# First panel pair behind two block norms on unnormalised tiles, the norm's factor applied to its results

## The chip, the cores and the metric

One core of one Trainium2 chip runs the whole program. The metric is the device time of one execution in microseconds (us). Each kernel is run several times and the median is compared.

## What is computed

Two transformer-like blocks work on 512 tokens of width 1024, in float32. The part that matters is in the second: a layer ends with a gated feed-forward block (down0 below), the next layer is a short convolution, and another feed-forward block follows (up1, down1). Each of them starts with a root-mean-square norm with a scale and a shift that come from a modulation vector:

```python
def rmsnorm(x, g):
    y = xf * lax.rsqrt(jnp.mean(xf * xf, axis=-1, keepdims=True) + NORM_EPS)
    return (y * g.astype(jnp.float32)).astype(x.dtype)

a = rmsnorm(h, norm1[i]) * (1.0 + sc1) + sh1
b_gate, c_gate, u = jnp.split(a @ w_in, 3, axis=-1)
h = h + g1 * ((b_gate * dwconv(c_gate * u, conv_w)) @ w_out)
n = rmsnorm(h, norm2[i]) * (1.0 + sc2) + sh2
g, u = jnp.split(n @ w_gate_up, 2, axis=-1)
h = h + g2 * ((jax.nn.silu(g) * u) @ w_down)
```

The factor of the norm belongs to the token, gain and scale to the channel of the input, so that (x * gain * (1 + scale) * r + shift) @ W = r * ((x * gain * (1 + scale)) @ W) + shift @ W.

## The kernel before, in words

All activations lie transposed: channels on the 128 partitions, tokens along the free axis. H holds the residual stream as 8 tiles of 128x512. A weight matrix is taken in panels of 128 output columns by up to 1024 input rows. Each panel is loaded by a DMA that SyncE issues into one of two slots of WS (`panel`, L667), and then split into a high and a low fp32r part: ScalarE copies (`split_panel`, L1508), VectorE subtracts (L2016), each in two halves of 128x512. SyncE loads a panel when both halves of the low split of the panel two before are done. Each product of float32 tiles is made of three fp32r matmuls: high input by low weights, low by high, high by high (`linear`, L854 to L867). A tile of output is 8 input tiles of 3 matmuls, 24 in all, or 66 in down0 and down1 with their 22 input tiles.

The order of the work is written out by hand, one program per engine with semaphores between them; there is no planner. `STAGES` (L48) lists the stages with their counts of panels and tiles. Around the change they are: up0 and down0, norm_e, conv_in (four passes of six panels: for j = 0 and 1 a c-gate panel, a u panel and a b-gate panel), conv_out (four passes of two), norm_f, up1 (22 passes of a gate panel and an up panel), down1. ada7a, ada7b and ada7c are modulation parts: VectorE multiplies and adds pieces of the modulation weights, TensorE sums the columns against ones (`add_beside`, L907, 8 matrix products that appear as 16 records), VectorE takes the result (`take_layer_part`, L2488).

A block norm runs as follows. For each of the 8 residual tiles VectorE updates H from the accumulator (L2474), ScalarE squares it (L1517), VectorE adds the squares up in SS (L2025). Behind the last one TensorE sums SS over the channels (`square_sum`, L914), ScalarE takes Ln and Exp (`root`, L1519) for the factor RS of each token, and `layer_norm` makes the eight normalised tiles: VectorE multiplies H by NS and RS (L2094), ScalarE adds the shift into the high part (L1554), VectorE makes the low part (L2088). The first two panels behind a norm go through `linear_pair` (L869): their weights lie in slots of their own (NH, NL), they use banks 2 and 3, and each normalised tile is multiplied by both panels as soon as it is there.

On VectorE, the low splits of the next stage's panels stand inside the queue of the stage's own work. In conv_in's first pass (L2749 on) VectorE, having made the norm, takes two modulation parts, clears CU, multiplies the two results of j = 0 (L2757), runs the three convolution taps (L2762, L2764), and only then splits panel 3. In up1's first pass it multiplies gate and up (L2730), makes the low part (L2732) and splits panel 3 at the head of the second pass. In down0 and conv_out, `residual_tile` (L2465) splits the next panel and then updates the residual tile.

Of the kernel before, what the change touches and what calls it, by code (L numbers as in the profile page):

```python
# [6 lines left out]
F32 = mybir.dt.float32  # L7
# [5 lines left out]
P = 128  # L13
# [54 lines left out]
    ("down0", 4, 6, 2, 0, 0),  # L68
    ("ada7a", 1, 0, 0, 1, 0),
    ("norm_e", 1, 0, 0, 1, 0),  # L70
    ("ada7b", 1, 0, 0, 1, 0),
    ("conv_in", 4, 6, 6, 0, 0),
    ("conv_out", 4, 2, 2, 0, 0),
    ("ada7c", 1, 0, 0, 1, 0),
    ("norm_f", 1, 0, 0, 1, 0),
# [244 lines left out]
def hybrid_then_diff_conv(nc, ins, consts, dist_rows, dist_table, out):  # L320
    with ExitStack() as ctx:
# [116 lines left out]
        A4H = sb("A4H", [P, KT, S], F32R, four)  # L438
        A4L = sb("A4L", [P, KT, S], F32R, four)
# [3 lines left out]
        YL = sb("YL", [P, KT, S], F32R, four)  # L443
        YT = sb("YT", [P, 2, S], F32, four)
        CU = sb("CU", [P, 2, S + 2], F32, four)
        CV = sb("CV", [P, 2, S], F32, four)
        four.close()
# [59 lines left out]
        f_hi, f_lo = sem("f_hi"), sem("f_lo")  # L507
        c_tap, cu_zero, out_kept, out_sent, last_sent = (sem(n) for n in ("c_tap", "cu_zero", "out_kept", "out_sent", "last_sent"))
# [308 lines left out]
        def _(pe):  # L817
# [51 lines left out]
            def linear_pair(a, hi, lo, base):  # L869
# [4 lines left out]
                for k in range(KT):  # L874
                    pe.wait_ge(ln_lo, base + k + 1)
                    for (wh, wl), b in tiles:
# [3 lines left out]
                        if k == KT - 1:  # L880
                            m.then_inc(w_used, 1)

# [558 lines left out]
            def ffn(l, count, base):  # L1441
                square_sum("norm_d" if l == 0 else "norm_f", count, 2 if l == 0 else 1)
                for a, _ in passes(pe, f"up{l}"):
                    if a.first():
                        linear_pair(a, A3H, A3L, base)
                    else:
                        linear(a, 0, 0, A3H, A3L)
                        linear(a, 1, 1, A3H, A3L)
# [31 lines left out]
            add_beside(At("ada7c"), 0, 12, SUM_BANKS[1])  # L1480
# [5 lines left out]
        def _(act):  # L1486
# [329 lines left out]
            def residual(stage, r, squared=True):  # L1816
                for a, more in passes(act, stage):
                    for t in range(2):
                        residual_tile(a, t, a.pg // 2, r, more, squared)
# [143 lines left out]
            def ffn(l, stage, L, shift, r, squared):  # L1963
                split(At(f"up{l}"), 1)
# [3 lines left out]
                for a, more in passes(act, f"up{l}"):  # L1968
                    if not a.first():
                        split(a, 1)  # L1970
                    panel_done(a, 0)
                    act.wait_ge(acc_free[acc(a, 1)], a.tile_round(1))
# [872 lines left out]
```

## Time and profile before

| | us |
|---|---|
| median of 3 runs | 1748.38 |
| lowest and highest | 1746.42, 1754.33 |
| the profiled execution | 1751.81 |
| its span in the trace | 1750.0 |
| TensorE busy | 1678.7 (96%) |
| VectorE busy | 976.1 (56%) |
| ScalarE busy | 678.1 (39%) |
| mean granted clock of TensorE | 0.976 of 2.4 GHz |

The span counts from the first to the last recorded instruction. Times in the trace are microseconds from the span's start. Where a row gives several instructions (x2), its duration is from the first's start to the last's end. The granted clock is in parts of 2.4 GHz: 1.00 is 2.4 GHz and 0.50 is 1.2 GHz.

### The profile page before, as it was taken

What the parts mean: (1) busy time and instruction counts of PE and PEld (TensorE: products, weight loads), DVE (VectorE), ACT (ScalarE), POOL (GpSimd) and SP (SyncE); (2) the same over time, 40 slices, a digit from 0 to 9 for tenths busy, and PEclk for the clock granted to TensorE, in tenths of its full rate; (3) what the DMA queues carried; (4) which work ended last, traced back from release to release, by engine and by line L of the source; (5) the groups of instructions that cost most, each with busy time, mean ns of one, the idle gap of its engine ahead of it and who ended that gap; (6) DMA issues with size and microseconds to landing.
All of it is one profiled execution on the core that took longest, in us unless ns stands there. A gap on an engine that the chain in (4) does not pass through costs nothing.

```text
span 1750.0 us, 22898 instructions
## 1 busy us (share of the span) xinstructions
PE 1678.7 (96%) x8888; PEld 1397.3 (80%) x8888; DVE 976.1 (56%) x1805; ACT 678.1 (39%) x1413; POOL 61.8 (4%) x120
## 2 busy tenths in 40 slices
PE   4899999999999999899999999999999899999999
PEld 2777777777999999777888888887888788888887
DVE  5667466766777766666555554345555533333332
ACT  3434556554455555554322323223222433333221
POOL 0000000000000000000000000000000000000000
PEclk9899998999999999998999999998999899999999
DMA  8886333313223131220666665433343233333332
GB/s 306 220 238 174 104 89 97 97 25 91 51 60 97 48 98 51 71 72 26 191 192 182 177 181 164 123 108 88 113 129 101 77 98 96 97 97 96 99 113 79
DMA packets 290215, 202.02 MB, mean 115 GB/s; under 512 B 76247, under 2 KB 272072, under 8 KB 289082
## 3 DMA queue, kind: packets, MB, share of 16 engines
q1 hardware_dynamic: 266942, 133.21, 27.3%
q0 software_dynamic: 15536, 56.37, 10.7%
q10 hardware_dynamic: 7628, 10.97, 1.9%
q8 instruction: 71, 1.16, 0.3%
q14 instruction: 38, 0.31, 0.1%
HBM read 197.33 MB, written 5.28 MB: 116 GB/s over the span
## 4 chain that ended last, share of the span: by engine, by line
PE 87%; DVE 6%; ACT 2%; issue 2%; DMA 2%; ACTq 1%; SPq 0%; DVEq 0%
PE PS L864 13%; PE PS L866 13%; PE PS L865 13%; PE PS L846 4%; PE PS L848 4%; PE PS L847 4%; PE PS L1285 3%; PE PS L1287 3%; PE PS L1286 3%; PE PS L1335 2%; PE PS L1094 2%; PE PS L1359 2%; PE PS L1068 1%; PE PS L1076 1%; PE PS L1347 1%
## 5 line engine op out<-in xcount | busy, mean ns | idle before, releaser
L2016 DVE TENSOR_TENSOR WL<-WS,WH 128x512 fp32r<-128x512 f32 x416 | 268.2, 687 | 256.5 <-ACT WH L1508 256.0
L1508 ACT ACTIVATE WH<-WS 128x512 fp32r<-128x512 f32 x416 | 237.8, 621 | 176.5 <-PE PS L848 135.0
L864 PE MATMUL PS<-A3H,WL 128*128 128x512 f32 x672 | 262.8, 391 | 0.2
L866 PE MATMUL PS<-A3H,WH 128*128 128x512 f32 x672 | 261.6, 389 | 0.0
L865 PE MATMUL PS<-A3L,WH 128*128 128x512 f32 x672 | 261.4, 389 | 0.0
L864 PEld LDWEIGHTS PS<-A3H,WL 128*128 128x128 f32 x672 | 126.1, 188 | 30.0 <-issue 4.5
L866 PEld LDWEIGHTS PS<-A3H,WH 128*128 128x128 f32 x672 | 126.1, 188 | 26.6
L865 PEld LDWEIGHTS PS<-A3L,WH 128*128 128x128 f32 x672 | 126.2, 188 | 25.8
L846 PE MATMUL PS<-GH,WL 128*128 128x512 f32 x352 | 137.4, 390 | 0.6 <-DVE WL L2016 0.6
L848 PE MATMUL PS<-GH,WH 128*128 128x512 f32 x352 | 137.0, 389 | 0.0
L847 PE MATMUL PS<-GL,WH 128*128 128x512 f32 x352 | 137.0, 389 | 0.0
L2045 DVE SCALAR_TENSOR_TENSOR AA<-AW,CS,AA 128x1024 f32<-128x1024 f32 x91 | 116.5, 1280 | 3.2
L2730 DVE TENSOR_TENSOR RAW<-SQ,PS 128x512 f32<-128x512 f32 x44 | 30.3, 688 | 136.9 <-PE PS L866 129.0
L1976 ACT ACTIVATE GH<-RAW 128x512 fp32r<-128x512 f32 x44 | 27.8, 632 | 194.9 <-DVE RAW L2730 194.9
L805 POOL DMA_DIRECT2D AW<-in_ada_w x96 | 50.7, 528 | 1144.7 <-DVE AA L2045 619.0
L1973 ACT ACTIVATE SQ<-PS 128x512 f32<-128x512 f32 x44 | 26.4, 600 | 139.3 <-PE PS L866 133.8
L846 PEld LDWEIGHTS PS<-GH,WL 128*128 128x128 f32 x352 | 66.1, 188 | 14.6 <-DVE WL L2016 1.0
L848 PEld LDWEIGHTS PS<-GH,WH 128*128 128x128 f32 x352 | 66.1, 188 | 13.7
L847 PEld LDWEIGHTS PS<-GL,WH 128*128 128x128 f32 x352 | 66.1, 188 | 13.6
L1094 PEld LDWEIGHTS PS<-VP,PT 128*128 128x128 f32 x432 | 61.5, 196 | 16.2 <-ACT PT L1705 9.4
L864 PE MATMUL PS<-A4H,WL 128*128 128x512 f32 x176 | 68.6, 390 | 0.0
L865 PE MATMUL PS<-A4L,WH 128*128 128x512 f32 x176 | 68.5, 389 | 0.0
(363 smaller groups left out, 3440.3 us busy)
## 6 DMA issues: line engine op xcount, KB each, us to landing
AW<-in_ada_w POOLq DMA_DIRECT2D x96, 512.0 KB, 4.1
WS<-in_ffn_w_gate_up SPq DMA_DIRECT2D x88, 512.0 KB, 4.6
WS<-in_ffn_w_down SPq DMA_DIRECT2D x32, 512.0 KB, 4.2
WS<-in_sc_w_in SPq DMA_DIRECT2D x24, 512.0 KB, 4.1
AB<-in_w_ada SPq DMA_DIRECT2D x8, 1024.0 KB, 15.8
WS<-in_w_in SPq DMA_DIRECT2D x32, 256.0 KB, 4.6
WS<-in_diff_w_qkv SPq DMA_DIRECT2D x64, 128.0 KB, 2.7
WS<-in_ffn_w_down SPq DMA_DIRECT2D x16, 384.0 KB, 3.5
```

Of the source, the lines that this page charges most:

```text
L846: mm(out_ap, WL[:, s, k, :], act_hi(k0 + k), start=start and k == ks[0], stop=False)
L847: mm(out_ap, WH[:, s, k, :], act_lo(k0 + k), start=False, stop=False)
L848: m = mm(out_ap, WH[:, s, k, :], act_hi(k0 + k), start=False, stop=stop and k == ks[-1])
L864: mm(PS[:, b, :], wl[:, k, :], hi[:, k, 0:S], start=(k == 0), stop=False)
L865: mm(PS[:, b, :], wh[:, k, :], lo[:, k, 0:S], start=False, stop=False)
L866: m = mm(PS[:, b, :], wh[:, k, :], hi[:, k, 0:S], start=False, stop=(k == KT - 1))
L1094: m = mm(PS[:, OB, c:c + HD], PT[:, v % 2, j * P:(j + 1) * P], VP[:, x, k0 // P + j, HD * g:HD * g + HD], start=(j == 0), stop=(j == n - 1))
L1285: mm(o, th[:, k, tok], wl, start=(k == 0), stop=False)
L1286: mm(o, tl[:, k, tok], wh, start=False, stop=False)
L1508: f(weights(p)[0][:, k, :], WS[:, p % 2, k, :], ACT.Copy).then_inc(w_hi, 1)
L2016: tt(lo[:, k, :], WS[:, p % 2, k, :], hi[:, k, :].bitcast(F32), ALU.subtract).then_inc(w_lo, 1)
L2045: stt(sums, src, CS[:, c:c + 1], sums, ALU.mult, ALU.add).then_inc(part_sum, 1)
```

## The change

In the two places where a norm follows a residual (norm_e in front of conv_in, norm_f in front of up1):

- While a residual stage runs, each of its finished tiles is also multiplied by the channel's factor NS and split into a high part (ScalarE) and a low part (VectorE): X4H and X4L for conv_in, A4H and A4L for up1. NS is computed in front of the residual stage.
- The first pair of panels is multiplied with these tiles (`ahead_pair`). Square sum, modulation sums and a bias sum are placed between its input tiles.
- The shift's share: during the low split of each of the two panels VectorE adds up weights times shift over the panel's 8 blocks (`bias_partial`, eight operations of 128x128); TensorE sums the result over partitions (`bias_sums`).
- The two results are multiplied by RS and the shift's share is added (`scaled_pair` on VectorE, a ScalarE pass with a bias).
- The low and high split of the second panel of each pair is moved in front of the last residual tile.
- The norm still makes its eight tiles, for all later panels; the third panel (`linear` with ln_lo) takes them one by one.
- The third modulation part (ada7c) moves from the end of conv_out into up1's pair, the others into conv_in's pair. The buffers are laid out anew for it.

```diff
+            def ahead_pair(a, hi, lo, base, beside):
+                for t in range(2):
+                    take_panel(a, t)
+                    wait(pe, acc_free[acc(a, t)], a.tile_round(t) - 1)
+                tiles = [(weights(a.panel(t)), bank_of(a, t)) for t in range(2)]
+                for k in range(KT):
+                    pe.wait_ge(x_lo, base + k + 1)
+                    for (wh, wl), b in tiles:
+                        mm(PS[:, b, :], wl[:, k, :], hi[:, k, :], start=(k == 0), stop=False)
+                        mm(PS[:, b, :], wh[:, k, :], lo[:, k, :], start=False, stop=False)
+                        m = mm(PS[:, b, :], wh[:, k, :], hi[:, k, :], start=False, stop=(k == KT - 1))
+                        if k == KT - 1:
+                            m.then_inc(w_used, 1)
+                    beside(k)
+            def bias_sums(n):
+                pe.wait_ge(bias_part, 16 * (n + 1))
+                for i in range(2):
+                    m = mm(PS[:, 6, i:i + 1], BP[:, i, :], ONES[:, 0:1], start=True, stop=True)
+                m.then_inc(bias_sum, 1)
...
+                def beside(k):
+                    if k == 1:
+                        square_sum("norm_f", count)
+                    elif k == 3:
+                        add_beside(At("ada7c"), 0, 12, SUM_BANKS[1])
+                    elif k == 5:
+                        bias_sums(1)
...
-                        linear(a, 0, 0, A3H, A3L)
+                        linear(a, 0, 0, A3H, A3L, ln_lo if l and a.i == 1 else None, base)
...
-            add_beside(At("ada7a"), 0, 10, SUM_BANKS[1])
-            square_sum("norm_e", 32, 1)
-            add_beside(At("ada7b"), 0, 11, 5)
+            def beside_conv(k):
+                if k == 1:
+                    square_sum("norm_e", 32)
+                elif k == 3:
+                    add_beside(At("ada7a"), 0, 10, SUM_BANKS[1])
+                elif k == 4:
+                    add_beside(At("ada7b"), 0, 11, 5)
+                elif k == 5:
+                    bias_sums(0)
             for a, _ in passes(pe, "conv_in"):
                 if a.first():
-                    linear_pair(a, A4H, A4L, 32)
+                    ahead_pair(a, X4H, X4L, 0, beside_conv)
                 for j in range(2 if a.first() else 0, 6):
-                    linear(a, j, j, A4H, A4L)
+                    linear(a, j, j, A4H, A4L, ln_lo if a.first() and j == 2 else None, 32)
...
                 if squared:
+                    if a.i == 3 and t == 1:
+                        split_panel(a.panel(2 * per + 1))
                     squares(a, t, 2 * a.i + (8 * r + t), one(H, a.i, 2, t))
...
+                            act.wait_ge(ln_scale, r + 1)
+                            f(squared[:, k, :], H[:, k, :], ACT.Identity, scale=NS[:, k:k + 1]).then_inc(x_hi, 1)
...
+                    if a.first() and j == 0:
+                        act.wait_ge(bias_in, 1)
+                        act.wait_ge(scaled, 1)
+                        f(SQ[:, 0, :], SQ[:, 0, :], ACT.Identity, bias=BC[:, 0:1]).then_inc(acc_free[acc(a, 0)], 1)
...
                     dve.wait_ge(w_hi, 2 * p + half + 1)
+                    for n in range(2):
+                        if half and p - AHEAD[1 + n] in (0, 1):
+                            bias_partial(n, p - AHEAD[1 + n], WS[:, p % 2, :, :], M2[:, 48 + 24 * n:56 + 24 * n])
                     tt(lo[:, k, :], WS[:, p % 2, k, :], hi[:, k, :].bitcast(F32), ALU.subtract).then_inc(w_lo, 1)
+            def bias_partial(n, i, w, shift):
+                before = 16 * n + 8 * i
+                for k in range(KT):
+                    if k == 0:
+                        ts(BP[:, i, :], w[:, k, :], shift[:, k:k + 1], None, ALU.mult).then_inc(bias_part, 1)
+                    else:
+                        dve.wait_ge(bias_part, before + k)
+                        stt(BP[:, i, :], w[:, k, :], shift[:, k:k + 1], BP[:, i, :], ALU.mult, ALU.add).then_inc(bias_part, 1)
...
+                if squared and a.i == 3 and t == 1:
+                    split_panel(a.panel(2 * per + 1))
...
+                            dve.wait_ge(x_hi, 8 * (r - 3) + k + 1)
+                            stt(squared[1][:, k, :], H[:, k, :], NS[:, k:k + 1], squared[0][:, k, :].bitcast(F32),
+                                ALU.mult, ALU.subtract).then_inc(x_lo, 1)
...
+            def scaled_pair(a, dst):
+                panel_done(a, 1)
+                tt(SQ[:, 0, :], PS[:, bank_of(a, 0), :], RS[:, 0, :], ALU.mult).then_inc(scaled, 1)
+                tt(RAW[:, 1, :], PS[:, bank_of(a, 1), :], RS[:, 0, :], ALU.mult).then_inc(acc_free[acc(a, 1)], 1)
+                dve.wait_ge(acc_free[acc(a, 1)], a.tile_round(1) + 1)
+                dve.wait_ge(acc_free[acc(a, 0)], a.tile_round(0) + 1)
+                stt(dst, RAW[:, 1, :], BC[:, 1:2], SQ[:, 0, :], ALU.add, ALU.mult).then_inc(paired, 1)
...
-            split(At("conv_in"), 1)
             split(At("conv_in"), 2)
```

## Rows read from the trace of the kernel before

**Rows 1.** The page, busy time by engine: us, share of the span, instructions.

```profile
PE 1678.7 (96%) x8888; PEld 1397.3 (80%) x8888; DVE 976.1 (56%) x1805; ACT 678.1 (39%) x1413; POOL 61.8 (4%) x120
```

**Rows 2.** The chain of waits in order of time: start, duration, engine, output, line.

```profile
1186.15 0.76 DVE H L2474
...
1372.30 0.76 DVE H L2474
...
1374.49 2.09 PE PS L919 x2
...
1378.05 0.76 DVE RAW L2094
```

**Rows 3.** Busy time by stretches: stretch, length, engines; then clock, DMA share, GB/s.

```profile
1186.13:1194.65 8.52, 5.80 (x34) 4.83 (x34) 7.56 (x14) 5.30 (x9) 0.53 (x1) 0.74 0.39 117
1372.27:1380.49 8.22, 3.74 (x17) 2.11 (x18) 6.37 (x13) 5.41 (x9) 0.00 (x0) 0.64 0.56 157
...
754.50:757.00 2.50, 0.00 (x0) 0.00 (x0) 2.47 (x5) 0.81 (x1) 0.00 (x0) 0.94 0.00 0
757.00:759.70 2.70, 2.69 (x6) 2.17 (x7) 1.15 (x2) 0.00 (x0) 0.00 (x0) 0.50 0.11 28
...
731.50:732.74 1.24, 0.04 (x1) 0.00 (x0) 0.02 (x1) 1.24 (x6) 0.00 (x0) 1.00 0.00 0
```

**Rows 4.** Timeline of TensorE, first products of the third panels: start, duration, instruction.

```profile
1208.33 0.39 PE L864 MATMUL PS<-A4H,WL 128*128 128x512 f32 x1
...
1393.46 0.39 PE L864 MATMUL PS<-A3H,WL 128*128 128x512 f32 x1
```

**Rows 5.** Timeline of TensorE: a square sum, and a modulation sum between products.

```profile
1188.34 1.13 PE L919 MATMUL PS<-SS,CN 128*128 128x512 f32 x2 [0.55 <-DVE SS L2025]
...
973.53 1.84 PE L894 MATMUL PS<-CN,AA 128*128 128x1 f32 x16
```

**Rows 6.** Groups of VectorE instructions by form: count, busy us, mean ns, idle before.

```profile
L2094 DVE SCALAR_TENSOR_TENSOR RAW<-H,NS,RS 128x512 f32<-128x512 f32 x32 | 23.7, 751 | 2.4 <-ACT RS L1524 1.5
...
L2094 DVE SCALAR_TENSOR_TENSOR RAW<-H,NS,RS 128x256 f32<-128x256 f32 x16 | 7.6, 484 | 0.7 <-ACT RS L1524 0.2
...
L2508 DVE TENSOR_TENSOR ROPE<-ANGLE,GD 128x128 f32<-128x128 f32 x8 | 1.7, 287 | 0.0
```

**Rows 7.** Timeline of VectorE: two neighbours without, then two with dependence.

```profile
1192.21 1.41 DVE L2094 SCALAR_TENSOR_TENSOR RAW<-H,NS,RS 128x512 f32<-128x512 f32 x2
...
1209.84 1.54 DVE L2764 SCALAR_TENSOR_TENSOR CV<-CU,VT,CV 128x512 f32<-128x512 f32 x2
```

**Rows 8.** Timelines of ScalarE, SyncE's queue and VectorE near the end of down0.

```profile
1178.50 1.15 ACT L1508 ACTIVATE NH<-WS 128x512 fp32r<-128x512 f32 x2 [0.67 <-DMA WS<-in_sc_w_in]
...
1178.67 0.37 SPq L672 DMA_DIRECT2D WS<-in_sc_w_in  x1
...
1179.16 1.29 DVE L2016 TENSOR_TENSOR NL<-WS,NH 128x512 fp32r<-128x512 f32 x2 [0.53 <-ACT NH L1508]
```

**Rows 9.** DMA issues from 1174 to 1190: count, KB each, median us to landing.

```profile
WS<-in_sc_w_in SPq DMA_DIRECT2D x3, 512.0 KB, 3.9
```

**Rows 10.** Timeline of VectorE, norm's end and first tile of conv_in.

```profile
1202.46 1.63 DVE L2088 SCALAR_TENSOR_TENSOR A4L<-RAW,M,A4H 128x512 fp32r<-128x512 f32 x2
...
1204.44 0.92 DVE L2747 MEMSET CU<- 128x1028 f32 x1 [0.17 <-issue]
1208.58 0.69 DVE L2757 TENSOR_TENSOR CU<-PS,SQ 128x512 f32<-128x512 f32 x1 [3.22 <-PE PS L879]
...
1211.41 1.29 DVE L2016 TENSOR_TENSOR WL<-WS,WH 128x512 fp32r<-128x512 f32 x2
```

**Rows 11.** Timeline of VectorE, end of conv_out and first tile of up1.

```profile
1366.85 0.75 DVE L2474 SCALAR_TENSOR_TENSOR H<-PS,M,H 128x512 f32<-128x512 f32 x1 [2.10 <-PE PS L866]
...
1368.90 1.29 DVE L2016 TENSOR_TENSOR NL<-WS,NH 128x512 fp32r<-128x512 f32 x2
...
1388.30 1.63 DVE L2088 SCALAR_TENSOR_TENSOR A3L<-RAW,M,A3H 128x512 fp32r<-128x512 f32 x2
...
1395.68 1.28 DVE L2016 TENSOR_TENSOR WL<-WS,WH 128x512 fp32r<-128x512 f32 x2
```

More of the change, by code:

```diff
@@ L437, in hybrid_then_diff_conv @@
         four = ExitStack()
[L438 to L439 removed]
+        X4H = sb("X4H", [P, KT, S], F32R, four)
+        X4L = sb("X4L", [P, KT, S], F32R, four)
         NH = sb("NH", [P, 2, 8, P], F32R, four)
@@ L443, in hybrid_then_diff_conv @@
         YL = sb("YL", [P, KT, S], F32R, four)
+        A4H = sb("A4H", [P, KT, S], F32R, four)
+        A4L = sb("A4L", [P, KT, S], F32R, four)
         YT = sb("YT", [P, 2, S], F32, four)
@@ L446, in hybrid_then_diff_conv @@
         CV = sb("CV", [P, 2, S], F32, four)
+        BP = sb("BP", [P, 2, P], F32, four)
+        BC = sb("BC", [P, 2], F32, four)
         four.close()
@@ L1441, in ffn @@
             def ffn(l, count, base):
-                square_sum("norm_d" if l == 0 else "norm_f", count, 2 if l == 0 else 1)
+                def beside(k):
[5 more added lines that the diff above has]
+                        bias_sums(1)
+                if l == 0:
+                    square_sum("norm_d", count, 2)
                 for a, _ in passes(pe, f"up{l}"):
-                    if a.first():
+                    if a.first() and l == 0:
                         linear_pair(a, A3H, A3L, base)
+                    elif a.first():
+                        ahead_pair(a, A4H, A4L, 8, beside)
                     else:
-                        linear(a, 0, 0, A3H, A3L)
+                        linear(a, 0, 0, A3H, A3L, ln_lo if l and a.i == 1 else None, base)
                         linear(a, 1, 1, A3H, A3L)
@@ L1963, in ffn @@
             def ffn(l, stage, L, shift, r, squared):
-                split(At(f"up{l}"), 1)
+                if l == 0:
+                    split(At("up0"), 1)
                 split(At(f"up{l}"), 2)
@@ L1995, in _ @@
                     f(YH[:, 2 * a.i + j, :], YT[:, j, :], ACT.Copy).then_inc(y_hi, 1)
-            residual("conv_out", 4)
-            ffn(1, "norm_f", 5, 72, 5, False)
+            residual("conv_out", 4, A4H)
+            ffn(1, "norm_f", 5, 72, 5, None)
         @block.vector
@@ L2719, in ffn @@
             def ffn(l, L, part, gain, r, squared):
-                split(At(f"up{l}"), 1)
+                if l == 0:
+                    split(At("up0"), 1)
                 split(At(f"up{l}"), 2)
-                layer_norm(L, L - 1, H, A3H, A3L, slice(0, S), M2[:, 8 * part + 8:8 * part + 16], M2[:, 8 * part:8 * part + 8], gain, 0)
+                layer_norm(L, L - 1, H, A3H, A3L, slice(0, S), None if l else M2[:, 8 * part + 8:8 * part + 16],
+                           M2[:, 8 * part:8 * part + 8], gain, 0)
+                if l:
+                    bias_taken(1)
+                    take_layer_part("ada7c", 0, 12, SUM_BANKS[1])
                 for a, more in passes(dve, f"up{l}"):
@@ L2773, in _ @@
             clear_squares(5)
-            residual("conv_out", 4, M2[:, 64:72])
-            take_layer_part("ada7c", 0, 12, SUM_BANKS[1])
-            ffn(1, 5, 9, V_N2 + 8, 5, False)
+            factors(M2[:, 80:88], V_N2 + 8)
+            residual("conv_out", 4, M2[:, 64:72], (A4H, A4L))
+            ffn(1, 5, 9, V_N2 + 8, 5, None)
             take_out(7)
```

86 lines of the change are left out of this document (58 added, 28 removed).

## The prediction

> **What bounds the kernel now.** The page's busy times come first: TensorE is busy for 96% of the span [rows 1], so time can only come from the places where it stands still or is paid at the lower clock. The chain of waits in order of time shows two of them where the change works. Behind the last product of down0 the chain leaves TensorE for a residual update at 1186.15, behind conv_out at 1372.30 [rows 2], and TensorE has its next product at 1194.65 and 1380.49 [rows 3]. What lies between is serial: residual update, square, sum, column sum on TensorE, Ln and Exp, the first normalised tile with its high and low part.
>
> The table by stretches shows the rest of the price. In both gaps TensorE does only column sums, and the granted clock falls to 0.74 and 0.64 [rows 3]. The first product is then at half rate: a pause of 2.50 us elsewhere is followed by 2.7 us at 0.50, where a pause of 1.24 us left the clock alone [rows 3]. The first products of the third panel stand at 1208.33 and 1393.46 [rows 4]. So from the last product to the end of the panel pair there are 22.2 and 21.2 us, where 48 products take 10.9: 24 take 5.44, the distance of two residual updates in conv_out (1366.85 [rows 11], 1372.30 [rows 2]).
>
> **How much could come back.** After the change the pair can start at once, but work that lay in the gap moves into it: the square sum (1.1 us for two records, [rows 5]), two modulation sums at conv_in and one at up1 (16 records each, 1.8 us, [rows 5]), and the bias sum, four such records, 0.5 us. A pair that never waits takes 10.9 + 1.1 + 3.6 + 0.5 = 16.1 us at conv_in and 10.9 + 1.1 + 1.8 + 0.5 = 14.3 us at up1. The ceiling is 6.1 + 6.9 = 13.0 us, 0.7% of the run. That needs VectorE to keep up, and I find that it doesn't.
>
> **The added work.** Each residual tile gains a ScalarE pass and a VectorE pass of 0.75 us; both fit in the slack of a tile (5.44 us of products at the shortest), so I cost them at nothing there, except where they stand in front of the split of the first up1 panel, below. If that cover were gone each would cost its 0.75 us. The weights of panels 0 and 1 gain a chain of eight 128x128 VectorE operations each, every one waiting for the one before. No row has this operation. A scalar_tensor_tensor of 512 columns takes 0.751 and one of 256 takes 0.484 [rows 6]: 1.04 ns a column, so 0.35 for 128, and 0.03 for the wait (two dependent taps of 0.75 fill 1.54 [rows 7]). With a cheaper first one that is 2.9 us per chain. Bounds: 128 columns as tensor_tensor without dependence 0.287 [rows 6], less the 0.08 by which unhindered neighbours overlap, gives 1.7 us; the 256-column row gives 4.1. I take 2.9, by the slope.
>
> Here a rule bears. In the rows, two VectorE passes of 0.75 that don't wait for one another fill 1.41 us, so the second starts 0.67 behind the first, and two dependent ones fill 1.54 [rows 7]. The Trainium skill, VectorE: DVE Perf Modes, section The DRAIN you can't avoid, says a semaphore between chained operations costs nothing extra. By that rule the chain would cost 2.1 us instead of 2.9 and the sum below would be 2.4 us lower; the trace disagrees, so I keep 2.9.
>
> **Conv boundary, step by step.** Panel 0's low split starts at 1179.16 [rows 8]: first half to 1179.8, chain to 1182.7, second half to 1183.4. Panel 1's load is issued at 1178.67 [rows 8] and lands 3.9 us later [rows 9], ScalarE's halves (1.15 for two [rows 8]) are ready at 1183.2 and 1183.8, VectorE: half 1184.1, chain 1187.0, half 1187.7. Two things queue behind it on VectorE: TensorE needs both panels complete, and the last residual update stands behind the split. TensorE starts at 1187.7 instead of 1194.65, after a pause of 1.6 us, which I take to leave the clock up. Panel 0's slot also comes free 2.9 us later, and with it the load of panel 2, which lands near 1187.3 and is wanted at 1189.8: hidden. Residual, square, sum take 2.2 (1186.15 [rows 2] to 1188.34 [rows 5]): ready at 1189.8, before two tiles of products (2.7 us) are through. The column sum ends at 1191.5, Ln and Exp take 1.4 (the sum's end at 1376.58 to 1378.05 [rows 2]), and the norm starts at 1192.9.
>
> The norm is unchanged, 11.9 us on VectorE (1378.05 [rows 2] to 1389.93 [rows 11]), and ends at 1204.8. TensorE finishes the pair at 1187.7 + 16.1 = 1203.8 and panel 2 at 1209.2. What is late next is **panel 3's low split**. It stands on VectorE behind the whole first tile: bias copy, two modulation takes and memset (now 1204.09 to 1205.36 [rows 10]; with a copy and a take more 1.9 us, to 1206.7), two products with the factor (1.35), the sum-and-product (0.8), three taps (2.1), then half a split (0.7): 1211.65. The taps' 2.1 lie between the product of 0.7 at 1208.58 and the split behind it, both in [rows 10]. Today the same split starts at 1211.41 [rows 10], its first half is there at 1212.1, and TensorE wants it at 1208.33 + 5.44 = 1213.8. Afterwards TensorE stands from 1209.2 to 1211.7 and then goes on 2.1 us earlier than now. **Gain 2.1 us**, where 6.1 were on offer.
>
> **Up1 boundary.** In conv_out a tile lasts only 5.44 us. Panel 0's split, at 1368.90 now [rows 11], starts 0.75 later behind the new pass, at 1369.7; half 1370.4, chain 1373.3, half 1374.0, panel 1: half 1374.7, chain 1377.6, half 1378.3. Panel 1's data are in by 1371, so here both chains lie on the path. The last product ends at 1372.27: TensorE pauses 6.0 us, and the last residual waits too. After such a pause the clock is low; as in the row of 2.7 us [rows 3] I take 3 us at half rate, a loss of 1.5. First two tiles to 1382.5, column sum 1383.6, Ln and Exp 1385.0, norm to 1396.9. Then copy and take 0.6, the two products 1.35, sum-and-product 0.8, high and low part of the output 1.4, half a split 0.7: panel 3 is ready at 1401.6. Today that split starts at 1395.68 [rows 11] and TensorE wants it at 1393.46 + 5.44 = 1398.9. TensorE's own side: 1378.3 + 14.3 + 1.5 + 5.44 = 1399.5, so it stands 2.1 us. **Loss 2.7 us.**
>
> The two pauses in front of panel 3 (2.5 and 2.1 us) lie between the 1.24 that left the clock and the 2.50 that lowered it; I count one of them, 1.5 us. Everything behind is bound by TensorE as before, and passes on what it is given.
>
> **Sum.** -2.1 + 2.7 + 1.5 = +2.1 us on the profiled execution's 1751.81 (span 1750.0, 1.8 around it), which was 3.4 above the median; on the median of 1748.38 it gives 1750.5. A measurement here tells about 0.5%, 8.7 us, from no change.
>
> **Rivals.**
> 1. *As forecast*, the wait moves from the norm to the split of panel 3 and to the weight chains: 1750.5. Chance 0.55, with costs between the bounds. For it: panel 3's split stands at 1211.41 today, its first half only 1.7 us ahead of need.
> 2. *The chains are cheap.* With 1.7 us each, panel 0's chain at conv_in is hidden behind the load, panel 1's gives back 1.2, up1's two give back 2.4, and the pause at conv_in is too short for the clock: 1750.5 - 3.6 = 1746.9, or 1745.4 if no clock is lost in front of panel 3. Chance 0.20. For it: the 0.287 of [rows 6]; against: that row has no dependence.
> 3. *It works in full*: VectorE reaches panel 3 in time, as would be if the sums in the pair left it slack. 1748.4 - 13.0 = 1735.4. Chance 0.05. Against: even with chains at zero the norm can't start before 2.2 us of residual, 1.1 of sum and 1.5 of roots behind the last product, and its 11.9 and the 7 us in front of the split end near 1210.
> 4. *Slower: TensorE's clock.* All four pauses (1.6, 6.0, 2.5, 2.1 us) are followed by half rate. The 1.6 us one decides: at half rate two tiles last until 1191.9, the norm starts 1.5 later and with it panel 3. Price 1.5 each for two more: 1753.5. With the 256-column price (1.2 more for three exposed chains, 3.6) it is 1757.1, still within 0.5%. Chance 0.17; past 0.5% it needs more, such as the load of panel 1 landing late behind POOL's transfer.
> 5. *The shift doesn't do what it says*: work is only exchanged and both products still wait for the norm (a wait left in the pair). That is the time of now plus the chains: 1748.4 + 2.9 x 3 = 1757. Chance 0.03. Against: the pair waits for the unnormalised tiles' semaphore alone.
>
> **How the numbers follow.** Slower by over 0.5% is a part of rivals 4 and 5: 0.06. Faster by over 0.5% is rival 3 and a tail of rival 2: 0.07. The rest, 0.87, can't be told from no change. The range reaches from rival 2 with 3 us for the scatter of the runs (1742) to rival 4 with both prices (1757).
>
> **What would show it.** Right: TensorE's first pair product some 1.6 and 6.0 us behind the last product of the stage before; a chain of 8 small VectorE operations near 2.9 us, twice, in front of the last residual; idle time on TensorE in front of the fourth panel of conv_in and up1, released by VectorE's low split; granted clock 0.5 for some 3 us at up1. Wrong: no idle in front of panel 3, a chain far from 2.9 us, or a changed time in conv_in's later passes or in down0, which I hold to be the same.

## The result, and the profile after

| | kernel before | changed kernel |
|---|---|---|
| median, first comparison (8 runs each) | 1749.46 us (1746.42 to 1754.33) | 1755.69 us (1754.24 to 1758.67) |
| median, measured again with other kernels | 1748.58 us (25 runs) | 1754.37 us (12 runs) |
| span of the profiled execution | 1750.0 us | 1754.2 us |
| mean granted clock of TensorE in it | 0.976 | 0.978 |

The ratio after to before is 1.0035, 95% interval [1.0022, 1.0048], and 1.0022 [1.0009, 1.0034] the second time. The change costs 4 to 6 us, two to three times the 2.1 us that the prediction added up. The ratios here and below are those of the record; they are not the quotients of the medians, and differ from them by up to 0.0014 (the medians of the second comparison alone would give 1.0033). The cost is within the 0.5% which the prediction called no change, and in its range (1742 to 1757), on the slow side of the 1750.5.

The busy times of the page hardly moved against [rows 1]; VectorE has 24 us more, which is the four chains (12 us) and the added pass of 0.75 us in each of 16 residual tiles. The page of the changed kernel:

```profile
span 1754.2 us, 22988 instructions
PE 1677.4 (96%) x8896; PEld 1396.1 (80%) x8896; DVE 999.7 (57%) x1859; ACT 688.3 (39%) x1429; POOL 61.9 (4%) x120
```

What moved is who keeps TensorE waiting. The table of waits of the changed kernel (engine, output, line, the releaser; then us in total, times, longest):

```profile
PE PS L899 <- DVE NL L2088: 8.1, 2, 5.8
PE PS L871 <- DVE WL L2088: 4.6, 2, 2.5
```

L899 is the first product of a pair, and L2088 the low half of a weight split on VectorE. So the pair no longer waits for a norm; at each of the two boundaries it waits for VectorE's weight work. The second line is the fourth panel (L871), which waits for its split in both stages. The timeline of TensorE in the changed kernel gives the places (start, duration, instruction, and in brackets the idle time before and what ended it):

```profile
1188.83 0.47 PE L899 MATMUL PS<-X4H,NL 128*128 128x512 f32 x1 [2.24 <-DVE NL L2088]
...
1212.96 0.47 PE L871 MATMUL PS<-A4H,WL 128*128 128x512 f32 x1 [2.51 <-DVE WL L2088]
...
1377.38 0.76 PE L899 MATMUL PS<-A4H,NL 128*128 128x512 f32 x1 [5.85 <-DVE NL L2088]
...
1401.34 0.47 PE L871 MATMUL PS<-A3H,WL 128*128 128x512 f32 x1 [2.08 <-DVE WL L2088]
```

The pauses of 2.24, 2.51, 5.85 and 2.08 us stand where the prediction put 1.6, 2.5, 6.0 and 2.1. What the clock did behind each is in the table by stretches (stretch, length, then PE, PEld, DVE, ACT, POOL busy with instructions; then the granted clock, DMA share, GB/s):

```profile
1188.83:1192.00 3.17, 3.17 (x13) 2.52 (x14) 2.47 (x4) 2.29 (x4) 0.00 (x0) 1.00 0.57 163
1212.96:1216.00 3.04, 3.04 (x13) 2.52 (x14) 2.34 (x5) 1.67 (x3) 0.00 (x0) 1.00 0.42 123
1377.38:1382.28 4.90, 4.90 (x12) 3.84 (x13) 3.02 (x5) 2.29 (x4) 0.00 (x0) 0.54 0.38 109
1401.34:1404.60 3.26, 3.26 (x10) 2.60 (x11) 1.75 (x3) 1.10 (x3) 0.00 (x0) 0.65 0.47 126
```

Only the two pauses at up1 were followed by the lower clock.

The timeline of VectorE in the changed kernel, behind [rows 8] and [rows 10], shows what the pair waits for: a half split, the first chain (0.28 and 2.67), two halves, the second chain (0.28 and 2.68), a half, and only then the residual update (L2570) that the norm needs:

```profile
1180.30 0.69 DVE L2088 TENSOR_TENSOR NL<-WS,NH 128x512 fp32r<-128x512 f32 x1 [1.18 <-ACT NH L1558]
1180.91 0.28 DVE L2097 TENSOR_SCALAR BP<-WS,M 128x128 f32<-128x128 f32 x1
1181.23 2.67 DVE L2100 SCALAR_TENSOR_TENSOR BP<-WS,M,BP 128x128 f32<-128x128 f32 x7
1183.82 1.29 DVE L2088 TENSOR_TENSOR NL<-WS,NH 128x512 fp32r<-128x512 f32 x2
1185.03 0.28 DVE L2097 TENSOR_SCALAR BP<-WS,M 128x128 f32<-128x128 f32 x1
1185.34 2.68 DVE L2100 SCALAR_TENSOR_TENSOR BP<-WS,M,BP 128x128 f32<-128x128 f32 x7
1187.93 0.68 DVE L2088 TENSOR_TENSOR NL<-WS,NH 128x512 fp32r<-128x512 f32 x1
1188.54 0.74 DVE L2570 SCALAR_TENSOR_TENSOR H<-PS,M,H 128x512 f32<-128x512 f32 x1
...
1194.17 1.41 DVE L2188 SCALAR_TENSOR_TENSOR RAW<-H,NS,RS 128x512 f32<-128x512 f32 x2 [0.43 <-ACT RS L1574]
...
1212.13 1.29 DVE L2088 TENSOR_TENSOR WL<-WS,WH 128x512 fp32r<-128x512 f32 x2
```

**How two executions are compared here.** The end of down0's last product came anywhere between 1180.4 and 1188.1 us in the single executions of this study, although none of the kernels differs much ahead of it. Absolute times say little, therefore; distances do. D stands for the end of down0's last product, C for that of conv_out's: the mark is 0.25 us behind the start of that product, about where the next one could start. (The end that the timeline shows is 0.14 later, so that a pause in its brackets is 0.14 shorter than the distance here: 2.24 and 2.38.) All are us from TensorE's timeline, one profiled execution each. "Pair" is the first product of the first pair of panels, "fourth" the first product of panel 3, and "the end" that of the whole span:

| kernel | D to pair | D to fourth | D to C | C to pair | C to fourth | up1's fourth to the end |
|---|---|---|---|---|---|---|
| before | 8.69 | 27.81 | 186.15 | 8.38 | 26.79 | 351.10 |
| changed | 2.38 | 26.51 | 184.94 | 5.99 | 29.95 | 352.86 |
| changed, again (e8) | 2.26 | 26.42 | 184.89 | 6.00 | 30.18 | 352.86 |
| e1_short_chain | 0.0 | 24.10 | 184.16 | 0.57 | 22.45 | 351.24 |
| e2_early_split | 2.53 | 24.01 | 182.92 | 5.99 | 27.16 | 351.14 |
| e3_both | 0.0 | 21.33 | 180.33 | 0.56 | 20.21 | 351.07 |
| e4_conv_only | 2.27 | 26.40 | 186.45 | 7.49 | 26.07 | 351.16 |
| e5_chain_behind_split | 0.0 | 22.96 | 182.16 | 3.08 | 25.44 | 351.15 |
| e6_chain_on_gpsimd | 0.0 | 22.18 | 182.16 | 4.52 | 26.64 | 351.13 |
| e7_shift_on_tensor | 1.68 | 22.70 | 183.91 | 1.68 | 20.97 | 351.37 |
| e9_mixed | 0.0 | 21.71 | 185.77 | 1.68 | 20.97 | 351.35 |
| e10_order_only | 0.0 | 26.37 | 186.47 | 3.08 | 27.04 | 352.78 |

(In e7 and e9, D to C holds 1.84 us of column sums that belong to up1. In e7 1.84 us of such sums for conv_in also stand ahead of D, in no column.)

Changed against before: conv_in with all of the block gains 186.15 - 184.94 = 1.2 us, the start of up1 loses 29.95 - 26.79 = 3.2, and the rest 352.86 - 351.10 = 1.8, which lies behind the 2.08 us pause, where the clock was 0.65. Together +3.7 us, a ratio of 1.0021; the two comparisons say 1.0022 and 1.0035.

### The profile page after: what moved, and what is told of

Read it like the earlier page. It is cut to its first block, busy times and chain, and to the rows that moved or that the text cites. A ratio compares the mean times of both kernels' runs of the same rounds, so it can differ in the third digit from the quotient of the medians.

```text
span 1754.2 us, 22988 instructions
## 1 busy us (share of the span) xinstructions
PE 1677.4 (96%) x8896; PEld 1396.1 (80%) x8896; DVE 999.7 (57%) x1859; ACT 688.3 (39%) x1429; POOL 61.9 (4%) x120
## 4 chain that ended last, share of the span: by engine, by line
PE 84%; DVE 9%; ACT 2%; issue 2%; DMA 2%; ACTq 1%; SPq 0%; DVEq 0%
PE PS L871 13%; PE PS L873 12%; PE PS L872 12%; PE PS L853 4%; PE PS L855 4%; PE PS L854 4%; PE PS L1315 3%; PE PS L1317 3%; PE PS L1316 3%; PE PS L1365 2%; PE PS L1124 2%; PE PS L1389 2%; PE PS L1098 1%; PE PS L1106 1%; PE PS L1377 1%
## 5 line engine op out<-in xcount | busy, mean ns | idle before, releaser
L2088 DVE TENSOR_TENSOR WL<-WS,WH 128x512 fp32r<-128x512 f32 x416 | 268.0, 686 | 249.9 <-ACT WH L1558 249.3
L871 PE MATMUL PS<-A3H,WL 128*128 128x512 f32 x672 | 263.5, 392 | 2.1 <-DVE WL L2088 2.1
L871 PEld LDWEIGHTS PS<-A3H,WL 128*128 128x128 f32 x672 | 126.5, 188 | 32.8 <-issue 6.9
L871 PE MATMUL PS<-A4H,WL 128*128 128x512 f32 x176 | 68.7, 390 | 2.5 <-DVE WL L2088 2.5
L873 PE MATMUL PS<-A4H,WH 128*128 128x512 f32 x176 | 68.5, 389 | 0.0
```

The source lines that it names most:

```text
L871: mm(PS[:, b, :], wl[:, k, :], hi[:, k, 0:S], start=(k == 0), stop=False)
L873: m = mm(PS[:, b, :], wh[:, k, :], hi[:, k, 0:S], start=False, stop=(k == KT - 1))
L2088: tt(lo[:, k, :], WS[:, p % 2, k, :], hi[:, k, :].bitcast(F32), ALU.subtract).then_inc(w_lo, 1)
```

## The experiments

In what follows the ratio is to the kernel before, measured beside it, with its 95% interval. "Against the changed kernel" is the difference of the ratios times 1748.6, taken from both measurements of the changed kernel (1.0022 and 1.0035). By the medians alone some differences come out up to 3 us otherwise; the conclusions don't turn on that.

### e1: the chain cut to one link

```diff
-                for k in range(KT):
+                for k in range(1):
```
(The semaphore's counts go with it. The result leaves out seven eighths of the shift's share in the pair.)

> Seven of the eight operations of each weights-times-shift chain are left out, so the shift's share of the two results is only that of the first input tile; nothing else changes. Theory A (VectorE's queue sets both ends of each boundary): at conv_in the last residual update starts 1.9 us earlier, at up1 4.7 us earlier, and the clock isn't lost at up1 (1.5): about 8 us less than the changed kernel, 1747.6. Pauses in front of panel 3 stay at 2.5 to 3 us. Theory B (the chains lie beside TensorE's work, and what costs is the sums put between the products): under 2 us.

Measured: 0.9971 [0.9960, 0.9983], 1742.90 us, 9 to 11 us below the changed kernel. Waits of TensorE in it:

```profile
PE PS L871 <- DVE WL L2088: 4.7, 2, 2.6
...
PE PS L899 <- DVE NL L2088: 0.4, 1, 0.4
```

The pair's wait is gone (0.4 is left of 8.1), up1's fourth panel comes 7.5 us earlier, conv_in's 2.4. The chains lie on the path, and the fourth panel's wait stays with its size (4.7 against 4.6): it only starts earlier.

### e2: the fourth panel's split moved ahead of the first tile

```diff
 on ScalarE, first tile of conv_in:
+                        split(a, 3)
                         act.wait_ge(bias_in, 1)
 on VectorE, behind the norm of conv_in, and at up1 behind its norm:
+            split(At("conv_in"), 3)
+                    split(At("up1", 1), 1)
```
(The later splits of the same panels go. Nothing is left out.)

> The split of panel 3 (high on ScalarE, low on VectorE) is moved from behind the first tile's own work to directly behind the norm, in both places; the chains stay. Theory A: both pauses in front of panel 3 go (2.5 and 2.1 us) and the 1.7 us at the lower clock behind the second; a wait of 0.5 us may come at panel 4 of conv_in: 5.8 us less than the changed kernel, 1750. Theory B (TensorE would wait for something else at once, such as the first tile's results): no change.

Measured: 0.9992 [0.9979, 1.0005], 1748.03 us, 5 to 7.5 us below the changed kernel. Waits of TensorE in it:

```profile
PE PS L899 <- DVE NL L2091: 8.3, 2, 5.9
...
PE PS L871 <- DVE WL L2091: 0.3, 1, 0.3
```

The mirror of e1: the pair waits as before, the fourth panel does not. Its place in the order was what made it late (the edit moves ScalarE's half of the split as well as VectorE's). Its gain in the table: 2.0 in D to C, 2.8 at up1, 1.7 behind it, together 6.5. Of the 2.8, 0.7 is the clock behind the long pause: 15 products fitted in the first 4.9 us of up1's pair here, 12 in the changed kernel.

### e3: both

The edits of e1 and e2 together, with the same part left out as in e1.

> Both edits: one operation of eight in each chain (the shift's share is that of the first input tile alone), and panel 3 split directly behind the norm. Theory A: TensorE alone sets the pace at both boundaries: pair start to fourth panel 16.1 + 5.4 us at conv_in and 14.3 + 5.4 at up1, no loss of clock: 15 us less than the changed kernel, 1740.6, which is more than the sum of the two edits alone (8 + 5.8). Theory B: the sum of both or less.

Measured: 0.9937 [0.9922, 0.9952], 1735.83 us, 15 to 17 us below the changed kernel. Waits of TensorE in it:

```profile
PE PS L899 <- DVE NL L2091: 0.4, 1, 0.4
...
PE PS L871 <- DVE WL L2091: 0.4, 1, 0.4
```

Both are gone. The fourth panel stands at 21.33 and 20.21 us, where the ceiling of the prediction has 16.1 + 5.4 = 21.5 and 14.3 + 5.4 = 19.7. The size came as expected, but it is **not more than the sum** of e1 and e2 (9.9 and 6.5 by the table, 16.1 here). At the conv boundary the two add up as far as the fourth panel (2.4 and 2.5, together 5.2); D to C shows only 0.8 for e1, because its execution lost 1.6 us at the lower clock behind that panel (see e4). At up1 the 1.7 us of lower clock behind the fourth panel, which each alone wins back, is there only once. In the total the 1.6 us that e1 lost and the 1.7 us that are counted twice nearly cancel.

### e4: the change at the conv boundary alone

```diff
-                    elif a.first():
-                        ahead_pair(a, A4H, A4L, 8, beside)
...
-                    for n in range(2):
+                    for n in range(1):
```
(Everything at norm_f and up1 as before.)

> The change is made at conv_in alone; norm_f, up1 and the third modulation part are as in the kernel before. Theory A (stage marks of the two traces: conv_in gains 1.2, up1 loses 3.2 and 1.7 by the clock): 4.9 us less than the changed kernel, 1750.8, and 1.2 less or equal to the kernel before. Theory B (the loss is spread, or comes from the added passes in the residual stages): between the two kernels, 2 us or more over the kernel before.

Measured: 1.0002 [0.9989, 1.0016], 1749.61 us. In relation to the changed kernel that is 3.5 to 6 us less. Up1's fourth panel is at 26.07, where before has 26.79 and the changed kernel 29.95: the loss is made at up1. Whether the conv half by itself gains its 1.2 us isn't to be seen; the interval ([0.9989, 1.0016], some 2 us to either side) holds both that and nothing. In its own profiled execution D to C is 186.45 and not 184.9, though the fourth panel came as early as in the changed kernel (26.40). The reason is behind that panel. The table by stretches, from e1, shows it, behind a pause of 2.60 us in front of the fourth panel of conv_in:

```profile
1206.45:1209.65 3.20, 3.20 (x9) 2.54 (x10) 2.50 (x5) 1.67 (x3) 0.00 (x0) 0.59 0.45 129
```

In the changed kernel the same place was at 1.00 behind 2.51 us. From that panel to C it is 158.3 us in the execution of before, 158.4 in both of the changed kernel, but 160.1 in e1, e4 and e10, with pauses of 2.60, 2.52 and 2.82 us: 1.6 us of lower clock that a pause of about 2.5 us brings in some executions and not in others. That is more than the change wins there.

### e8: the changed kernel once more

> The changed kernel itself, on the chip of this group, to compare the other runs with it directly. Theory A and B alike: 1.0035 of the kernel before, within the interval of the first measurement.

Measured: 1.0022 [1.0009, 1.0034], 1754.37 us. The distances repeat within 0.25 us (table), so that one profiled execution tells them, apart from the 1.6 us that the clock takes or leaves (e4). The total lies 0.0013 lower than the first time, at the edge of that interval.

### e5: the chain behind its panel's whole split, with e2's order

```diff
                 for half in range(2):
                     ...
-                    for n in range(2):
-                        if half and p - AHEAD[1 + n] in (0, 1):
-                            bias_partial(n, p - AHEAD[1 + n], WS[:, p % 2, :, :], M2[:, 48 + 24 * n:56 + 24 * n])
+                for n in range(2):
+                    if p - AHEAD[1 + n] in (0, 1):
+                        bias_partial(n, p - AHEAD[1 + n], WS[:, p % 2, :, :], M2[:, 48 + 24 * n:56 + 24 * n])
```
(And in the load of panels 2 and 3 a wait until the chain has read the panel's slot; e2's edits too. Nothing is left out.)

> Panel 3 split directly behind the norm as before, and all eight operations of each chain kept on VectorE, but behind both halves of the low split, not between them; SyncE loads the next panel of the slot only when the chain is done. The output is complete. Theory A: TensorE no longer waits for the chains directly but for the square sum, which is as late as in the changed kernel at conv_in (a wait of 1.3 us there) and the pair at up1 starts 3 us earlier, then waits 2 us: about 10 us less than the changed kernel, 6 more than with short chains. Theory B (only the amount of VectorE work counts, not its order): 7.5 less, as with the early split alone.

Measured: 0.9962 [0.9947, 0.9977], 1744.35 us, 10 to 13 us below the changed kernel, and **below the kernel before** with nothing left out. The longest wait that is left at a pair is the one chain in front of up1's second panel:

```profile
PE PS L902 <- DVE NL L2091: 2.9, 1, 2.9
```

At conv_in the pair starts without a wait: the second chain stands behind the split that TensorE needs. It still stands in front of the residual update, though, and so of the sum of squares, and for that TensorE waits inside the pair:

```profile
1187.48 0.70 PE L952 MATMUL PS<-SS,CN 128*128 128x512 f32 x1 [1.37 <-DVE SS L2120]
```

These 1.37 us are most of what puts the fourth panel at 22.96 and not at e3's 21.33.

### e10: e5's order of the chain, without e2

> The chains behind both halves of the low split, panel 3's split left where the change has it. The output is complete. Theory A (VectorE's queue sets the fourth panel): at conv_in the pair starts at once but the fourth panel starts at 26.4 us behind the last product as before; at up1 the norm starts 3 us earlier, the fourth panel at 27 instead of 30: 3 to 5 us less than the changed kernel, 1.000 of the kernel before. Theory B (the pauses in front of the pair are the loss): both gaps in front of the pair shrink by 5 us in all, and so does the time, with the clock 7 us.

Measured: 1.0004 [0.9991, 1.0016], 1750.30 us, 3 to 5 us below the changed kernel. The fourth panel of conv_in stays at 26.37 although the pair starts 2.4 us earlier, and up1's comes 2.9 earlier (27.04). So at conv_in the start of the pair is worth nothing as long as the fourth panel's split is late: the norm and the first tile on VectorE set its time. (The norm starts 7.59 us behind D, in the changed kernel 7.72.)

At up1 it isn't the residual update that came earlier: it starts 5.69 us behind C in both kernels, as both chains stand in front of it either way. What came earlier is TensorE's sum of squares, which stands behind the pair's first two tiles of products. The changed kernel, then e10:

```profile
1377.08 0.74 DVE L2570 SCALAR_TENSOR_TENSOR H<-PS,M,H 128x512 f32<-128x512 f32 x1
...
1382.28 1.02 PE L949 MATMUL PS<-SS,CN 128*128 128x512 f32 x2
...
1375.27 0.74 DVE L2573 SCALAR_TENSOR_TENSOR H<-PS,M,H 128x512 f32<-128x512 f32 x1
...
1377.46 1.12 PE L952 MATMUL PS<-SS,CN 128*128 128x512 f32 x2 [0.36 <-DVE SS L2117]
```

Behind C that is 10.89 us and 7.88. In the changed kernel the squares were ready some 3 us before TensorE, which had started the pair late and at the lower clock, came to them; in e10 TensorE is there first and waits 0.36. The norm follows the sum (it starts 13.40 and 10.50 behind C), and with it the fourth panel. So at up1 the late start of the pair did cost: through the place of the sum of squares in TensorE's own order, which Theory B had in part right.

### e6: the chain on GpSimd, with e2

```diff
+                pool.tensor_tensor(t, w, shift..., ALU.mult).then_inc(bias_part, 1)
+                for step, h in enumerate((4, 2, 1)):
+                    pool.wait_ge(bias_part, before + step + 1)
+                    pool.tensor_tensor(..., t[:, 0:h, :], t[:, h:2 * h, :], ALU.add)
```
(One product over the whole panel, then three halvings; nothing of this is left on VectorE. The load of the next panel waits for it.)

> Panel 3 split directly behind the norm, and the chains made by GpSimd instead of VectorE: one product over 8 blocks and three halving sums per panel. The output is complete. Theory A: as fast as with the chains cut to an eighth (0.9937 of the kernel before, 1736 to 1738), if GpSimd takes under some 5 us per panel. Theory B (GpSimd is slower than 8 us per panel, or slows VectorE's passes beside it): the bias sum or the load of panel 2 becomes late and over half of the gain is gone.

Measured: 0.9974 [0.9961, 0.9987], 1744.91 us. Against e2 (0.9992) it gains 0.0018, where cutting the chain to an eighth (e3) gains 0.0055: two thirds are gone (by the distances in the table more, as 1.3 of 9.5 us are left). VectorE's groups by form, from 1174 to 1187 us in e6 (busy us, mean ns, idle before):

```profile
L2116 DVE TENSOR_TENSOR NL<-WS,NH 128x512 fp32r<-128x512 f32 x4 | 5.6, 1460 | 1.4 <-ACT NH L1586 1.4
L2130 DVE TENSOR_TENSOR SS<-SS,SQ 128x512 f32<-128x512 f32 x1 | 1.8, 1757 | 0.7 <-ACT SQ L1595 0.7
...
L2597 DVE SCALAR_TENSOR_TENSOR X4L<-H,NS,X4H 128x512 fp32r<-128x512 f32 x1 | 1.2, 1209 | 0.0
L2586 DVE SCALAR_TENSOR_TENSOR H<-PS,M,H 128x512 f32<-128x512 f32 x1 | 0.8, 751 | 0.5 <-PE PS L883 0.5
```

and the same group in the changed kernel, from 1180 to 1192 us:

```profile
L2088 DVE TENSOR_TENSOR NL<-WS,NH 128x512 fp32r<-128x512 f32 x4 | 2.7, 686 | 1.2 <-ACT NH L1558 1.2
```

GpSimd's timeline in e6 covers that stretch:

```profile
1173.92 1.89 POOL L835 TENSOR_TENSOR CV<-WS,M 128x1024 f32<-128x1024 f32 x1 [18.45 <-DMA WS<-in_sc_w_in]
1175.89 2.77 POOL L838 TENSOR_TENSOR CV<-CV 128x512 f32<-128x512 f32 x2
1178.74 0.79 POOL L838 TENSOR_TENSOR BP<-CV 128x128 f32<-128x128 f32 x1
1179.67 2.16 POOL L835 TENSOR_TENSOR CV<-WS,M 128x1024 f32<-128x1024 f32 x1
1181.91 2.43 POOL L838 TENSOR_TENSOR CV<-CV 128x512 f32<-128x512 f32 x2
```

A half split takes 1460 ns instead of 686, the sum 1757, while GpSimd computes. The residual update at 1180.55, which reads PSUM and one operand of SBUF, took its usual 751 in the middle of GpSimd's product of 1179.67. VectorE's load was moved off its queue and came back as longer instructions. Most of the loss is at up1, where the pair waits for the stretched splits of its panels, 4.4 us instead of the changed kernel's 5.8:

```profile
PE PS L927 <- DVE NL L2116: 4.4, 1, 4.4
```

### e7: the shift's sum on TensorE, with e2

```diff
-                pe.wait_ge(bias_part, 16 * (n + 1))
-                for i in range(2):
-                    m = mm(PS[:, 6, i:i + 1], BP[:, i, :], ONES[:, 0:1], start=True, stop=True)
+                pe.wait_ge(w_loaded[p % 2], loads_of(p))
+                for k in range(KT):
+                    m = mm(PS[:, 6, i:i + 1], WS[:, p % 2, k, :], M2[:, 48 + 24 * n + k:49 + 24 * n + k],
+                        start=(k == 0), stop=(k == KT - 1))
```
(Called at the end of down0 and of conv_out, for one panel ahead of the last products and for the other behind them, in front of the pair; the chain on VectorE is removed, and the load of the next panel waits for the sums.)

> Panel 3 split directly behind the norm, and weights times shift taken by TensorE from the unsplit panels, 16 records of one column per panel in place of the chain. The output is complete. Theory A: VectorE is as free as with short chains, TensorE has 3.2 us more per boundary: 6.4 us over the version with short chains and early split, 1742. Theory B (these sums fit where TensorE would pause): 1738.

Measured: 0.9961 [0.9945, 0.9977], 1744.13 us, 11 to 13 us below the changed kernel. TensorE's timeline in e7 has the price of one panel's sums:

```profile
1184.33 1.84 PE L916 MATMUL PS<-M,WS 128*128 128x1 f32 x16
```

TensorE pays 2 x 1.84 us per boundary on the path for 2 x 2.95 us off VectorE. At up1, where both chains were exposed, the fourth panel comes 9.0 us earlier (20.97; with the sums in front of C, 7.1). At conv_in, where e5's chains cost little, it loses: D to C without up1's sums is 182.1, as in e5 (182.2), and 1.84 us of its own sums stand ahead of D. The gain over e5 at up1, 25.44 - 20.97 - 1.84 = 2.6 us, and this loss nearly cancel, and the totals are equal.

### e9: e5 at conv_in, e7 at up1

> The cheaper way at each place: at conv_in the chains on VectorE behind both halves of the split and the square sum one input tile later; at up1 weights times shift by TensorE from the unsplit panels; panel 3 split directly behind the norm in both. The output is complete. Theory A: at conv_in the wait for the square sum (1.4 us) goes, fourth panel 21.5 us behind the last product of down0; at up1 as with the sums on TensorE (21.0 behind the last product, 1.8 us in front of it). 9 us less than the kernel before, 1739.5. Theory B (what is won at the pair is lost at a later panel of conv_in): as the two parents, 0.996.

Measured: 0.9966 [0.9952, 0.9979], 1743.32 us, not below its parents (0.9962, 0.9961): what the rival of that expectation said. TensorE's timeline in e9, fifth panel of conv_in:

```profile
1213.69 0.47 PE L875 MATMUL PS<-A4H,WL 128*128 128x512 f32 x1 [1.97 <-DVE WL L2101]
```

and the stretch behind it:

```profile
1213.69:1217.00 3.31, 3.31 (x10) 2.69 (x11) 1.75 (x3) 1.09 (x3) 0.00 (x0) 0.68 0.47 136
```

The fourth panel stands at 21.71, nearly the ceiling; one panel later TensorE waits 1.97 us for the next split, and goes on at a lower clock. D to C without up1's sums is 183.9, against 182.2 in e5: those 1.8 us take two thirds of the 2.6 us that e7's form wins at up1 (25.44 against 20.97 + 1.84). From the fourth panel to C, without up1's sums, e9 has 162.2 us and e5 159.2: 1.4 us of the difference is the longer pause (1.97, where e5 has 0.58), and the rest, 1.6, is the size of what the clock took elsewhere behind such a pause. VectorE's backlog is passed on by one panel.

## Why the prediction was right, and where it was off

**Ceiling: right, and shown.** The prediction had 13.0 us on offer (1735.4). e3, in which VectorE has an eighth of the chains and no late split, ran at 1735.83, 13.0 below the kernel before by the medians, 12.4 by the distances and 11.0 by the ratio.

**That VectorE's queue takes it away: right.** e1 takes one cause out (-9 to -11 us), e2 the other (-5 to -7.5), e3 both (-15 to -17). What lies between the changed kernel and the ceiling at the two boundaries is in these two.

**The chain at 2.9 us: right.** VectorE's groups in the changed kernel, 1180 to 1192 us:

```profile
L2100 DVE SCALAR_TENSOR_TENSOR BP<-WS,M,BP 128x128 f32<-128x128 f32 x14 | 4.9, 352 | 0.5
```

352 ns each, where the slope of [rows 6] gave 0.35. Seven of them fill 2.67 us, so they start 0.386 apart, (2.67 - 0.352) / 6, which is 0.03 behind the end of the one before, as [rows 7] had it; unhindered neighbours overlapped by 0.08. So dependence costs an estimated 0.11 us a link here (the overlap is that of other operations; no run has this chain without its waits). The rule that a semaphore between chained operations costs nothing extra (the Trainium skill, VectorE: DVE Perf Modes, The DRAIN you can't avoid) isn't borne out in this sense: by it the links would start some 0.27 apart, an estimate from 0.352 - 0.08. Rival 2, which needed 1.7 us a chain, falls with the measured 2.95.

**Conv boundary: gain 2.1 predicted, 1.2 measured.** The step that failed is "I cost them at nothing there": the added ScalarE and VectorE passes in the residual tiles. They lie in the slack of a tile only as long as nothing on the queue behind them is due. Here the split of the down0 panel that is two ahead of conv_in's first stands behind such a pass, and SyncE issues the load of conv_in's first panel when that split is done. Before, then changed:

```profile
1174.56 0.37 SPq L672 DMA_DIRECT2D WS<-in_sc_w_in  x1
...
1175.72 0.37 SPq L679 DMA_DIRECT2D WS<-in_sc_w_in  x1
```

That is 11.40 us ahead of D before and 10.73 in the changed kernel, 0.67 later. Relative to D the first conv split starts at 1180.30 - 1186.45 = -6.15, where [rows 8] has 1179.16 - 1185.96 = -6.8, 0.65 later. ScalarE's row in the changed kernel names the load as what it waited for:

```profile
1179.64 1.15 ACT L1558 ACTIVATE NH<-WS 128x512 fp32r<-128x512 f32 x2 [1.31 <-DMA WS<-in_sc_w_in]
```

The wait there was 0.67 us before. So the pair started after a pause of 2.24 us instead of 1.6, and the norm and the fourth panel 0.8 later (26.51 where 25.7 was forecast, 1211.65 - 1185.96). The step from the pass to the load is read from the traces alone: no run took the pass away by itself.

**Up1 boundary: loss 2.7 predicted, 3.2 measured.** Every step of the order held: pause 5.85 (6.0), the fourth panel's 2.08 (2.1). Mis-sized was the half rate behind the long pause: 12 products took 4.90 us at a clock of 0.54, where 2.72 is the time at full rate, a loss of 2.2 instead of 1.5. It was 2.2 in e8 too, but 1.5 in e2 behind the same pause, so the size differs between executions. (The prediction's own steps on VectorE add up to 1401.75 and not to its 1401.6; that changes nothing.)

**The clock behind the pauses in front of the fourth panels: one of two, right by count, and in part luck.** 352.86 - 351.10 = 1.8 us are lost behind up1's pause, against the 1.5 counted; behind conv_in's the clock stayed in the changed kernel. That it was one was a choice and not worked out, and e1, e4 and e10 show the other outcome at conv_in with the same kind of pause.

**The sum** was -2.1 + 2.7 + 1.5 = +2.1; measured are -1.2 + 3.2 + 1.8 = +3.7. All three terms erred to the same side, by 0.9, 0.5 and 0.3 us. The forecast held because its range, 15 us wide, is much wider than the effect; of the difference itself it had between a third and a little over half.

**Rivals 3, 4 and 5.** Rival 3 needed VectorE to be in time for the pair and for the fourth panel; with the whole chain on VectorE no run has both; e3, which leaves work out, and e7, which pays for it on TensorE, do. Rival 4 had the clock lower behind all four pauses; it was so behind two, the 2.24 us in front of the pair left it at 1.00, and so the 1.5 us that this rival puts on the norm at conv_in are not there. In number alone its 1753.5 is nearer to the 1754 to 1756 measured than the 1750.5 is. Rival 5 falls with the timeline: the pair starts at 1188.83, the norm at 1194.17.

**What stays open**: whether the conv half alone gains its 1.2 us (e4 can't tell it from nothing), the load's delay by the added pass, what decides the clock behind a pause of 2 to 3 us, and why the first comparison of the changed kernel has a ratio 0.0013 above the second, where the medians give 1.0036 and 1.0033.

## What to carry to other kernels

When a wait between two engines is removed, write down the queue of the engine that did the work in the gap, in order, up to the next thing it owes to the other: the time gained is that of the first item that comes too late, and here an operation with no hurry (the chain) and one that was urgent (the fourth panel's split) stood in the wrong order; the order alone turned a ratio of 1.0022 to 1.0035 into 0.9962 (e5). Write down the order on the waiting engine too: at up1 the sum of squares that the norm needs stood behind two tiles of products that started late, and the norm came 3 us later for it (e10). Work that is "hidden in the slack" also delays the reads that free a buffer, and so a load. Moving the load off the queue isn't enough: on GpSimd it slowed VectorE's own instructions, on TensorE it cost two thirds of the time that it took off VectorE, and where nothing was late any more up to the fourth panel the wait came back one panel later (e9).

## What the runs showed of the hardware

**Pauses of TensorE near 2 us do not decide the clock by their length.** 2.09 us (e1, up1's fourth panel), 2.24 and 2.51 (changed kernel) were followed by a granted clock of 1.00, which is the level of 2.4 GHz; 1.97 (e9), 2.08 (changed kernel), 2.50 [rows 3] and 2.60 (e1) by 0.50 to 0.68 over some 3 us, that is by products at the level of 1.2 GHz for most of the stretch. Even the same pause at the same place had both outcomes: 2.52 us in front of conv_in's fourth panel was followed by 1.00 in e8 and by 0.72 in e4. What decides it no run here shows. The stretch behind e1's 2.09:

```profile
1389.00:1392.40 3.40, 3.40 (x15) 2.81 (x16) 1.71 (x3) 1.05 (x3) 0.00 (x0) 1.00 0.52 152
```

The price was 1.6 us at conv_in (e1, e4, e10) and 1.7 to 1.8 at up1 (changed kernel, e8, e10).

**GpSimd's tensor_tensor can more than double VectorE's passes with two operands in SBUF**: 686 to 1460 ns for a half split, while the pass that reads PSUM and one operand in SBUF kept its 751. Two half splits in a row even filled 4.08 us in one place near the end of conv_out, against 1.28 for the two of the next panel, when GpSimd stood idle. The Trainium skill, SBUF — State Buffer, section SBUF: two separate sides, says that a VectorE operation with two SBUF inputs and a GpSimd operation that reads SBUF lock each other out of a shared pair of ports for a whole instruction; the trace agrees, as far as the mean durations can show it.
